# Normalizing the first input token-major: the head of a two-layer hybrid block is rebuilt around TensorE transposes

## The reference

```python
mod = (c_act @ ada_w[l] + ada_b[l])             # six vectors of 1024; shift_m, scale_m are the first two
h = rms_norm(x, mix_pre_g[l]) * (1.0 + scale_m) + shift_m
proj = h @ w_in[l]                              # 1024 -> 1792: k, q, v, x_lru, gate
```

## Time and profile before

| | us |
|---|---|
| median of 3 runs (1143.95 to 1145.02) | 1144.2 |
| the profiled execution, its own time | 1144.63 |
| its span in the trace | 1142.8 |
| TensorE busy | 1116.1 (98%) |
| VectorE busy | 803.2 (70%) |
| ScalarE busy | 567.4 (50%) |

### The profile page before, as it was taken

One profiled execution on the slowest core, in us unless ns is written; L12 is line 12 of the kernel. 1 busy time (PEld: TensorE's weight loads), 2 busy tenths in 40 slices (PEclk: granted clock), 3 DMA queues, 4 the chain that ended last, 5 costly groups with the idle time before them and its releaser, 6 DMA issues.

```text
span 1142.8 us, 14253 instructions
## 1 busy us (share of the span) xinstructions
PE 1116.1 (98%) x5638; PEld 936.3 (82%) x5638; DVE 803.2 (70%) x1229; ACT 567.4 (50%) x958; POOL 51.9 (5%) x110
## 2 busy tenths in 40 slices
PE   6999999999999999999999999999999999999997
PEld 6986777988888888888889778898888888888886
DVE  7999987776678876588576897777643655356545
ACT  4488948644124422244387895774422434134431
POOL 3100110000111011000000000000000000000000
PEclk7999999999999999999999999999999999999999
DMA  9853273334675547643232422323322332233231
GB/s 355 333 216 111 93 275 130 116 106 148 235 266 195 179 157 272 203 153 128 74 111 79 89 74 74 107 79 102 102 92 92 101 102 75 93 120 102 92 92 74
DMA packets 49284, 159.88 MB, mean 140 GB/s; under 512 B 9409, under 2 KB 9665, under 8 KB 49217
## 3 DMA queue, kind: packets, MB, share of 16 engines
q1 hardware_dynamic: 33968, 118.57, 30.6%
q0 software_dynamic: 10368, 37.75, 9.9%
q10 hardware_dynamic: 4880, 2.64, 0.9%
HBM read 156.83 MB, written 2.11 MB: 139 GB/s over the span
## 4 chain that ended last, share of the span: by engine, by line
PE 82%; DVE 7%; ACT 5%; DMA 3%; issue 2%; SPq 0%; DVEq 0%; ACTq 0%
PE ps L1834 48%; PE ps L1859 33%; DMA sb_raw<-in_w 2%; DVE sb_wL L1147 1%; DMA sb_vw<-in_ada 1%; ACT sb_wH L604 1%; DVE sb_x L1225 1%; PE ps L1947 1%; ACT sb_sq L736 1%; DVE sb_y L1192 1%; PE ps L2124 0%; ACT sb_I L835 0%; DVE sb_y L1199 0%; DVE sb_y L1239 0%; DVE sb_xc L1454 0%
## 5 line engine op out<-in xcount | busy, mean ns | idle before, releaser
L1834 PE MATMUL ps<-sb_hH,sb_wH 128*128 128x512 f32 x832 | 325.7, 391 | 0.3 <-DVE sb_R L1776 0.3
L1834 PE MATMUL ps<-sb_hL,sb_wH 128*128 128x512 f32 x832 | 323.9, 389 | 0.0
L1834 PE MATMUL ps<-sb_hH,sb_wL 128*128 128x512 f32 x832 | 323.9, 389 | 0.0
L1147 DVE TENSOR_TENSOR sb_wL<-sb_raw,sb_wH 128x1024 fp32r<-128x1024 f32 x182 | 221.2, 1220 | 87.1 <-ACT sb_wH L604 86.9
L604 ACT ACTIVATE sb_wH<-sb_raw 128x1024 fp32r<-128x1024 f32 x182 | 189.6, 1053 | 161.2 <-DMA sb_raw<-in_w 161.0
L1859 PE MATMUL ps<-sb_wH,sb_mH 128*128 128x512 f32 x512 | 202.5, 396 | 3.6 <-DVE sb_wL L1147 2.7
L1859 PE MATMUL ps<-sb_wL,sb_mH 128*128 128x512 f32 x512 | 199.7, 390 | 0.0
L1859 PE MATMUL ps<-sb_wH,sb_mL 128*128 128x512 f32 x512 | 199.6, 390 | 0.0
L1834 PEld LDWEIGHTS ps<-sb_hH,sb_wH 128*128 128x128 f32 x832 | 156.2, 188 | 37.6 <-issue 3.6
L1834 PEld LDWEIGHTS ps<-sb_hH,sb_wL 128*128 128x128 f32 x832 | 156.2, 188 | 32.8
L1834 PEld LDWEIGHTS ps<-sb_hL,sb_wH 128*128 128x128 f32 x832 | 156.2, 188 | 31.7
(11 more groups left out here) (222 smaller groups left out, 1135.0 us busy)
## 6 DMA issues: line engine op xcount, KB each, us to landing
sb_raw<-in_w SPq DMA_DIRECT2D x182, 512.0 KB, 3.5
sb_adaw<-in_ada POOLq DMA_DIRECT2D x42, 512.0 KB, 4.7
sb_stage<-in_ada SPq DMA_DIRECT2D x24, 512.0 KB, 14.3
sb_vw<-in_ada POOLq DMA_DIRECT2D x20, 512.0 KB, 5.2
sb_raw<-in_w SPq DMA_DIRECT2D x8, 384.0 KB, 14.3
sb_stage<-in_ada POOLq DMA_DIRECT2D x6, 512.0 KB, 3.8
sb_x<-in_x SPq DMA_DIRECT2D x4, 512.0 KB, 5.9
sb_x<-in_xt SPq DMA_DIRECT2D x4, 512.0 KB, 6.6
```

The lines of the kernel that those rows point to most:

```text
L1147: TT(low_of(n), raw_of(n), high_of(n).bitcast(fp32), ALU.subtract).then_inc(w_lo, 1)
L1834: return nc.tensor.matmul(out, a, b, start=start, stop=stop, **kw)
```

## The change

x is loaded once, token-major. ScalarE squares each token tile with a running sum (one column per tile), takes the root, VectorE takes the reciprocal and scales tiles 0 to 2, ScalarE scales tile 3; the scaled tiles (first) lie in scr, vw, work and gw. TensorE transposes them, four 128 x 128 blocks per kt, into bank 6, which is the only buffer: the transposes of kt + 1 stand in the middle of the 24 hH products of kt and wait until ScalarE has read bank 6 twice for kt. ScalarE makes both hH and the fp32 tile rt from bank 6, as gain times value plus shift; VectorE only subtracts. shift_sums(1) moves into kt 0, behind its hH products. The first half of kt 6 and 7 is no longer taken chunk by chunk but kt 6 for all chunks, then kt 7. The Exp of the softplus moves behind kt 2, the sine and cosine tables behind ScalarE's work of kt 3. The load of gw moves behind the last transpose, and the second load of x is gone.

```diff
-            for h in range(4):
-                sp.dma_start(x[:, h * part:(h + 1) * part], A["x"][:, h * part:(h + 1) * part]).then_inc(x_in[h], 16)
+            for t in range(QT):
+                sp.dma_start(x_tile(t), A["xt"][tile_of(t), :]).then_inc(x_in[t], 16)
...
-            sp.wait_ge(presq_used, 3)
-            sp.dma_start(gw[:, :, :], A["gw"][0]).then_inc(gw_in, 16)
...
-            sp.wait_ge(ada_used, 11)
-            sp.wait_ge(shift_mm, 4)
+            rows_used(6)
...
-            sp.wait_ge(tmp_ready, KT)
-            for t in range(QT):
-                sp.dma_start(x_tile(t), A["xt"][tile_of(t), :]).then_inc(xt_in, 16)
+            sp.wait_ge(first_turned, KT)
+            sp.dma_start(gw[:, :, :], A["gw"][0]).then_inc(gw_in, 16)
...
+            act.wait_ge(consts, 3)
+            fetch_sqrt()
+            def first_square(t):
+                act.wait_ge(x_in[t], 16)
+                nc.scalar.activation(first[t], x_tile(t), ACT.Square, accum_out=xsum[:, t:t + 1]).then_inc(first_sum, 1)
+            def first_root(t, total):
+                act.wait_ge(first_sum, total)
+                nc.scalar.activation(sd8[:, t:t + 1], xsum[:, t:t + 1], ACT.Sqrt, bias=eps,
+                                     scale=1.0 / D).then_inc(first_sd, 1)
+            first_square(0)
+            first_root(0, 1)
+            first_square(1)
+            first_root(1, 2)
             act.wait_ge(csil_mm, 1)
             nc.scalar.activation(csb[:, :], bank(6, 2), ACT.Copy).then_inc(csb_ready, 1)
+            first_square(2)
+            first_root(2, 3)
+            first_square(3)
+            first_root(3, 4)
+            act.wait_ge(first_rs, 4)
+            nc.scalar.activation(first[3], x_tile(3), ACT.Copy, scale=rs8[:, 3:4]).then_inc(first_hat[3], 1)
...
                 nc.scalar.activation(slab_of(wH, kt), slab_of(raw, kt), ACT.Copy).then_inc(slab_hi, 1)
+                act.wait_ge(first_turned, kt + 1)
+                act.wait_ge(shift_ready, kt + 1)
+                if kt >= 4:
+                    act.wait_ge(lo_ready, kt - 3)
+                shift, gain = mod[:, 0, kt:kt + 1], fac[:, 0, 0, kt:kt + 1]
+                nc.scalar.activation(hH[:, kt, :], bank(6), ACT.Identity, bias=shift, scale=gain).then_inc(hi_ready, 1)
+                nc.scalar.activation(rt(kt), bank(6), ACT.Identity, bias=shift, scale=gain).then_inc(tmp_ready, 1)
+                if kt == 2:
+                    softplus_exp()
                 if kt == 3:
                     rope_tables()
...
+            def first_scaled(t):
+                dve.wait_ge(first_sd, t + 1)
+                nc.vector.reciprocal(rs8[:, t:t + 1], sd8[:, t:t + 1]).then_inc(first_rs, 1)
+                if t < QT - 1:
+                    dve.wait_ge(first_rs, t + 1)
+                    TS(first[t], x_tile(t), rs8[:, t:t + 1], None, ALU.mult).then_inc(first_hat[t], 1)
...
             for kt in range(KT):
                 dve.wait_ge(stage_in[2 * kt], 16)
                 dot_unit(stage[:, 2 * kt, :], 1, kt)
                 dve.wait_ge(ada_used, used)
+                V.mark(TS(fac[:, 0, 0, kt:kt + 1], mod[:, 1, kt:kt + 1], gain_pre[:, kt:kt + 1], gain1[:, kt:kt + 1],
+                          ALU.mult, ALU.add))
                 if kt in PE_SHIFT:
+                    slab_low(kt)
                     dve.wait_ge(shift_mm, PE_SHIFT.index(kt) + 1)
                     sums = bank(7)[:, 8 + kt:9 + kt]
                 else:
+                    dve.wait_ge(stage_in[2 * kt + 1], 16)
+                    dot_unit(stage[:, 2 * kt + 1, :], 0, kt)
                     dve.wait_ge(ada_used, used)
                     sums = mod[:, 0, kt:kt + 1]
+                self_wait()
                 TT(mod[:, 0, kt:kt + 1], sums, bias_col(0, kt, 1), ALU.add).then_inc(shift_ready, 1)
+                if kt not in PE_SHIFT:
+                    slab_low(kt)
                 dve.wait_ge(hi_ready, kt + 1)
-                STT(out=hL[:, kt, :], in0=rt(kt), scalar=mod[:, 0, kt:kt + 1], in1=hi_of(hL)[:, kt, :],
-                    op0=ALU.add, op1=ALU.subtract).then_inc(lo_ready, 1)
+                dve.wait_ge(tmp_ready, kt + 1)
+                TT(hL[:, kt, :], rt(kt), hi_of(hL)[:, kt, :], ALU.subtract).then_inc(lo_ready, 1)
                 if kt == 2:
                     reduce_angle(1.0)
                     TS(ang, ang, PI, -PI, ALU.min, ALU.max).then_inc(ang_ready, 1)
+                    dve.wait_ge(sp_exp, 1)
+                    link(TS(sp1[:, :, :], sp2[:, :, :], 2.0, None, ALU.add))
+                    nc.vector.reciprocal(sp1[:, :, :], sp1[:, :, :]).then_inc(sp_recip, 1)
...
+            def first_transposes(kt):
+                if kt:
+                    pe.wait_ge(tmp_ready, kt)
+                for t in range(QT):
+                    if kt == 0:
+                        pe.wait_ge(first_hat[t], 1)
+                    last = nc.tensor.transpose(bank(6)[:, t * P:(t + 1) * P], first[t][:, kt * P:(kt + 1) * P], ident[:, :])
+                last.then_inc(first_turned, 1)
...
                     for c in range(GRP):
                         a, al = block_pair(c, kt)
+                        if c == GRP // 2:
+                            first_transposes(kt + 1)
...
+                    if kt == 0 and 1 in PE_SHIFT:
+                        shift_sums(1)
...
+                first_transposes(KT - 1)
                 for h in range(2):
+                    for kts in ([KT - 2], [KT - 1]) if h == 0 else ([KT - 2, KT - 1],):
+                        for c in range(GRP):
+                            for kt in kts:
...
             pe.wait_ge(csb_ready, 1)
-            norm_cols()
-            norm_spread(0, 6)
-            shift_sums(1)
+            first_transposes(0)
```

More of the change, by code:

```diff
@@ L184, in build @@
         sqb = [sq[:, :], work[:, SEQ:2 * SEQ]]
-        presq = [scr[:, :], vwf, work[:, :], gw[:, :, :].rearrange("p a b -> p (a b)")]
+        first = [scr[:, :], vwf, work[:, :], gw[:, :, :].rearrange("p a b -> p (a b)")]
         EARLY = range(2 * KT, 3 * KT)
@@ L493, in early_fill, with rows_used @@
                 sp.dma_start(early_slots[i], A["ada"][EARLY[i]]).then_inc(unit_in[i], 16)
-            sp.wait_ge(ada_used, 2)
+            def rows_used(kt):
+                sp.wait_ge(ada_used, 2 * (kt + 1) - sum(1 for s in PE_SHIFT if s <= kt))
+                if kt in PE_SHIFT:
+                    sp.wait_ge(shift_mm, PE_SHIFT.index(kt) + 1)
+            rows_used(0)
             early_fill(0)
             early_fill(1)
-            sp.wait_ge(ada_used, 5)
+            rows_used(2)
             early_fill(4)
@@ L683, in _, with softplus_exp @@
             nc.scalar.activation(ctmp, craw, ACT.Exp, scale=-1.0).then_inc(c_exp, 1)
[L684 to L687, removed]
+            act.wait_ge(consts, 3)
[11 more added lines that the diff above has]
+            first_root(1, 2)
             act.wait_ge(csil_mm, 1)
             nc.scalar.activation(csb[:, :], bank(6, 2), ACT.Copy).then_inc(csb_ready, 1)
[L690 to L696, removed]
+            first_square(2)
[4 more added lines that the diff above has]
+            nc.scalar.activation(first[3], x_tile(3), ACT.Copy, scale=rs8[:, 3:4]).then_inc(first_hat[3], 1)
+            def softplus_exp():
+                act.wait_ge(params_in, 16)
+                lam = par[:, :, COLS["lam"]:COLS["lam"] + LT]
+                S.mark(nc.scalar.activation(sp1[:, :, :], lam, ACT.Abs))
+                self_wait()
+                nc.scalar.activation(sp2[:, :, :], sp1[:, :, :], ACT.Exp, scale=-1.0).then_inc(sp_exp, 1)
             def rope_tables():
@@ L1286, in _ @@
                 dve.wait_ge(ada_used, used)
[L1287 to L1299, removed]
-                STT(out=rt(kt), in0=xt(kt), scalar=fcol, in1=bank(6), op0=ALU.mult, op1=ALU.mult).then_inc(tmp_ready, 1)
+                V.mark(TS(fac[:, 0, 0, kt:kt + 1], mod[:, 1, kt:kt + 1], gain_pre[:, kt:kt + 1], gain1[:, kt:kt + 1],
+                          ALU.mult, ALU.add))
                 if kt in PE_SHIFT:
+                    slab_low(kt)
                     dve.wait_ge(shift_mm, PE_SHIFT.index(kt) + 1)
@@ L2032, in pair_passes, with norm_spread @@
                             token_products(l, stage, fh, t, kt, kt == 0, ready if t == 0 else None)
-            def norm_cols():
-                pe.wait_ge(ssq_ready, 1)
-                for t in range(QT):
-                    last = mm(bank(7)[:, t:t + 1], ssq[:, t * P:(t + 1) * P], ones[:, 0:1], True, True)
-                last.then_inc(cols_ready, 1)
-            def norm_spread(m, b, rs=rs8):
-                if m:
-                    pe.wait_ge(g_copied, m * LT)
-                pe.wait_ge(rs_ready, m + 1)
+            def norm_spread(m, b, rs):
+                pe.wait_ge(g_copied, m * LT)
+                pe.wait_ge(rs_ready, m)
                 for t in range(QT):
@@ L2434 @@
         "in_w": stream, "in_w0": slabs, "in_ada": ada, "in_gw": gw, "in_par": par,
```

(1 more changed line is left out.)

60 lines of the change are left out of this document (24 added, 36 removed).

## The result

The changed kernel takes 1148.99 us (median of 5 runs, 1147.82 to 1151.29) against 1144.2 (median of 5, 1143.57 to 1145.97): a ratio of 1.0041, 95% interval [1.0028, 1.0054]. It is slower by 4.8 us; 1148.8 was forecast. The profiled execution is the shortest of the five, 1147.82 us with a span of 1146.0, 3.2 us above the one of before. Two of the ten runs of experiment e1 fell into a slower state of the chip (1240.58 and 1393.01 us, mean granted clock 0.85 and 0.75) and are left out everywhere.

What follows compares the result with a forecast made beforehand. TensorE bounds the old head; after the change VectorE's chain of rounds, waiting on ScalarE and the moved sums, ends it at 68.7 against 64.10 us. So 1144.63 + 4.6 = 1149.2, or 1148.8 against the median; range 1142.5 to 1152.2.

Steps and rivals of the forecast that it cites:

- The start: TensorE's first group of products in the head starts at 17.5 us (17.0 to 18.3), 4 us earlier than before.
- The transposes: Four added transposes per kt on TensorE cost 0.42 to about 0.5 us a set; seven sets inside the group, 3.5 us.
- The new latency: VectorE's rounds wait for ScalarE's hH and rt: even kt 5.0 us, odd 4.9, losing 1.1 in each of four rounds.
- Rival 4: ScalarE's pair out of PSUM is cheaper, by the skill's figure: 2.5 us less, 1146.3; counted within the main chance of 0.55.
- The place of shift_sums(1): Sums moved into TensorE's group end at 25.0 us; VectorE idles 3.7 us in round 1, starts round 2 at 27.35.
- a rise before 21 us: Sign against the prediction: TensorE's clock, expected to rise 5.4 us after the first product, rises before 21 us.
- rival 2: Clock full from the group's start or soon after: shift sums end 2.3 us sooner, 1146.5 us; chance 0.13.
- The rope tables and the slab of kt 4: Tables made on ScalarE behind round 3 move hH of kt 4 to 45.2 us rather than 44.0.
- TensorE's waits: TensorE waits 2.1 us for the kt 3 shift, and again for hL of kt 7, from 60.4 to 62.2 us.
- Rival 1: TensorE stays the head's bound, VectorE-ScalarE rounds hide behind it: head end 65.0, 1145.1 us; chance 0.17.
- Table load: Extra Exp load on ScalarE behind kt 2, 1.28 us without cover, hides while VectorE reduces angles; nothing added.
- Nothing absorbs the shift: The 4.6 us delay at the head's end, about 64 us, arrives whole at the kernel's end.

Runs made afterwards that it cites:

- e1: Changed kernel with the shift sum of kt 1 back on VectorE: 1144.48 us, ratio 1.0009 to the kernel before.
- e2: Changed kernel with VectorE making the low part of h one scale row later: 1144.14 us, ratio 1.0010 to the kernel before.
- e5: Changed kernel with the sine and cosine tables back ahead of ScalarE's hH of kt 3: 1146.61 us, ratio 1.0024 to the kernel before.
- e3: Changed kernel with each of the head's transposes issued twice: 1148.72 us, ratio 1.0055 to the kernel before.
- e7: Changed kernel with shift sum 1 on VectorE, low parts one scale row later and tables ahead of hH of kt 3: 1142.73 us, ratio 0.9989.
- after_again: The changed kernel, unedited, run once more on another chip: 1148.32 us, ratio 1.0039 to the kernel before.
- e6: Changed kernel with kt 6 and 7 of the first half chunk by chunk again: 1150.38 us, ratio 1.0054 to the kernel before.
- e10: Kernel before (x feature-major) plus zero products ahead of the group and the kt 6 and 7 split: 1143.51 us, ratio 1.0000.
- e4: Changed kernel with 19 zero products between the first transposes: 1145.81 us, ratio 1.0031 to the kernel before.
- e9: Changed kernel with the second load of x put back: 1148.19 us, ratio 1.0037 to the kernel before.
- e8: Changed kernel with low parts later, shift sums 1 and 3 on VectorE, angles behind round 5, tables ahead of kt 6, zero products: 1138.33 us, ratio 0.9946.

## Why the prediction was right, point by point

**The start.** 17.5 us was forecast, 17.16 came (17.2 to 17.5 over the runs). What the sum had too long is above all the way to VectorE's first dot, 13.8 in the sum, 13.27 in the trace.

**The transposes.** 0.42 to 0.5 us a set; 0.44 came.

**The new latency.** ScalarE's pair is 0.78 and 0.77 us, and an even round from 50.69 to 55.80, an odd one from 45.97 to 50.69: 5.1 and 4.7 us, 5.0 and 4.9 forecast. Rival 4 is out: every one of the 16 took 0.76 to 0.78 us. The smaller fixed cost from PSUM that the Trainium skill states ("VectorE: DVE Perf Modes", section on the TRN2 errata), 0.57 us by an estimate from it, did not show in this instruction with its two columns. e2 then showed what the latency costs by hiding it.

**The place of shift_sums(1)** is the step whose size was off. The sum let the clock rise 5.4 us after the group's first product, as before; it rose after 3.4 (2.9 to 5.1 over the nine runs in which the group began at half clock). Counting from the first product was the mistake: in each of these nine the clock had fallen ahead of the group, at 13.5 to 15.7 us, and the half level lasted 6.8 us from there (13.7 to 20.6 in after), whenever the products began. The forecast had named a rise before 21 us as a sign that it is wrong. It came at 20.6, so that sign is there: the mechanism held, but its clock term was wrong, by 2 us of half clock or 1 us of time. The sums ended at 23.9, not 25.0, VectorE's wait was 3.15 (3.7 forecast), and every round behind stands 1.0 to 1.6 us early: 26.37, 35.25, 39.93, 45.97, 50.69, 55.80 against 27.35, 36.25, 41.15, 47.4, 52.3, 57.3. That is half of rival 2, and most of the 1.4 us by which the head ended early (67.30 against 68.7). The rest is rounds a little shorter. e1 confirms the mechanism: without the moved sums, 2.6 us come back.

**The rope tables and the slab of kt 4** were forecast to delay round 4 by 1.2 us, and did, by 0.8: VectorE waits 1.6 us in it (1.16 for the slab, 0.44 for rt) where an even round waits 0.8 for rt anyway. e5 gives those 0.8 us back at the head's end.

**TensorE's waits**: ahead of kt 3 2.1 forecast, 1.96 measured; inside kt 7 1.8 and 1.43. Rival 1, no waits and TensorE the bound, is out for the change as made, but not by much: e3 shows about 1.15 us of room, and e2 and e7, with the latencies hidden, run to rival 1's pattern (its 65.0 against 65.05 and, with the sums back on VectorE, 62.59).

**Table load.** It took 1.28 us at 30.90, and VectorE asked for the Exp's result only at 34.93: the cover named in the forecast, VectorE's angles, was there. The order that the Trainium skill advises ("ScalarE: Activation LUTs", section on table sets) would have saved the load, and no time.

**Nothing absorbs the shift.** Shown: 1078.70 us behind the head in both traces, and 1076.9 to 1078.6 in the ten other traces with the token-major head, whose spans moved with the head's end.

**The number itself is better than its working.** The sum gave +4.6 and the medians say +4.8, but the trace that I can read shows +3.2, since the profiled runs, both times, were the shortest of their set. The four other runs of the first set are 0.3 to 3.5 us longer, and none of them was traced. What the traces do show of such differences lies behind the head. The two profiled runs of the changed kernel end their heads at 67.30 and 67.32 us and are 1.8 us apart behind them (1078.7 and 1076.9). In the first TensorE waits for the low part of a weight slab, in after_again it does not, since ScalarE begins to round that slab at 162.53 instead of 164.04:

```profile
166.48 0.50 PE L1883 MATMUL ps<-sb_wH,sb_mH 128*128 128x512 f32 x1 [1.43 <-DVE sb_wL L1171]
```

And a stretch of 3.4 us at half clock near 140 us, worth 1.7 us, stands in six of the thirteen traces (before, after, after_again, e3, e6, e10), and in none of the seven others. Here is the one of after:

```profile
140.00:143.40 3.40, 3.40 (x12) 2.08 (x12) 3.37 (x6) 2.70 (x3) 0.00 (x0) 0.50 0.00 0
```

Whether the longer runs had more of these is not shown. Another candidate of the right size is a second fall of the clock inside the head, behind a wait of TensorE (1.7 us in e4 and in e6). The spreads do not decide: without a long wait ahead of kt 3 they are 2.1 us (e1, eight runs), 2.0 (e2, ten) and 2.9 (e7, eleven), with it 4.7 (after_again, six) and 4.4 (e5, ten), but also 1.4 (e6, four); and the kernel before, which has no such wait, spread by 3.6, 6.3 and 7.1 us in its sets of 17 to 21 runs. The longest run of the first set, 1151.29 us, has the same mean clock, 0.994, as the shortest. The cause stays open, and that +4.6 and +4.8 lie so close is in part luck.

## What to carry to other kernels

When a step moves from one engine to two in relay, write down who waits for the second one and put an independent instruction of that engine between request and use; here one dot of distance in VectorE's queue was worth 2.3 us, and a reduction moved behind products that run at half clock cost 2.6. A change can be right in its idea and lose by its order, so try its parts in other positions before dropping it. And put a wait of TensorE into a sum with its length, and into the range with the half clock that may follow: here 1.7 us behind two of the seven waits of 1.95 us or more inside the group.

## What was not expected of the hardware

- The clock fell to half behind waits of 1.96 us (e4, for 3.4 us) and 3.21 us (e6, for 3.4 us), with TensorE busy without a gap when it fell; a like wait of 1.95 or 1.96 us ahead of kt 3 in after, after_again, e5, e6 and e9 had no such sequel. In e10 it fell during a set of shift sums of 128x1 products at 19.0, 1 us behind a gap of 0.96.
- The rise did not keep its distance from the group's first product: it came 2.9 to 5.1 us after it for nearly the same instructions. The half level ahead of it had the same length, 6.8 us, in all nine runs; what moved was the fall, between 13.5 and 15.7 us, in or behind gaps of 0.9 to 1.6 us between TensorE's first transposes. In a head whose second round waits for TensorE this alone moves the end by about 1 us.
- With 19 products with a zero tile, in stretches where TensorE waited, the clock was full over the whole start in e4 and e8, where it was half in the nine others; they cost no time: the group began at 17.23 and 17.26 us, as without them. In e10 products of this kind, in other places, did not do it.
